# Two decoder layers on one core: finer signals at stage hand-overs, and merged rows turned in two steps

## The reference

```python
for l in range(DEPTH):
    h = rms_norm(x, norm_mix[l])
    # projections of h; y_a: block attention, y_b: state space layer + GLU
    o_g = gated_delta_rule(q_g, k_g, v_g, log_decay, beta)
    o_g = rms_norm(o_g, gdn_norm[l]) * silu(z_g)
    y_c = o_g @ w_up_gdn[l]
    merged = sigmoid(gate_a) * y_a + sigmoid(gate_b) * y_b + sigmoid(gate_c) * y_c
    x = x + merged @ w_out[l]
    x = x + cross_attention(rms_norm(x, norm_xa[l]), rms_norm(mem, norm_mem[l]), ...)
    h = rms_norm(x, norm_ffn[l])
    x = x + (swiglu(h, ...) if l % 2 == 0 else moe_swiglu(h, router, ...))
return rms_norm(x, norm_final)
```

## Time and profile before

| what | value |
|---|---|
| runs, median (lowest to highest) | 1812.19 us (1810.71 to 1813.0), 3 runs |
| the profiled execution | 1812.14 us |
| its span, first to last instruction | 1810.4 us |
| TensorE busy | 1739.8 us, 96% |
| VectorE busy | 1404.4 us, 78% |
| ScalarE busy | 1053.2 us, 58% |
| HBM moved | 239 GB/s over the span |

### The profile page before, as it was taken

The page is one execution under the profiler, slowest core; times in us unless marked ns, Lnnn a source line. Parts: engine busy times, 40 slices in busy tenths (PEclk is TensorE's granted clock), DMA queues, the critical chain, the costliest instruction groups (busy, mean ns, idle before and its releaser), DMA issues. The chain is left out here.

```text
span 1810.4 us, 23711 instructions
## 1 busy us (share of the span) xinstructions
PE 1739.8 (96%) x9509; PEld 1408.4 (78%) x9509; DVE 1404.4 (78%) x1765; ACT 1053.2 (58%) x1212; POOL 157.9 (9%) x211
## 2 busy tenths in 40 slices
PE   7999989999999999999899899999999999999997
PEld 5687767687888788776677788888888888888885
DVE  5678679665555467976877588989898989999996
ACT  4234555465443522454645667777777868777775
POOL 7330002000000215000010010000000000000020
PEclk9999999999999989999999999999999999999999
DMA  8334521357462544443214679999999999999993
GB/s 258 132 119 169 175 98 67 117 209 249 146 209 93 157 140 140 140 163 116 94 48 173 222 291 390 379 390 378 390 375 389 371 389 373 391 376 390 365 398 141
DMA packets 219155, 434.92 MB, mean 240 GB/s; under 512 B 19164, under 2 KB 61800, under 8 KB 219048
## 3 DMA queue, kind: packets, MB, share of 16 engines
q1 hardware_dynamic: 212664, 419.45, 64.2%
q0 software_dynamic: 3520, 11.76, 1.7%
q10 hardware_dynamic: 2864, 2.23, 0.4%
HBM read 422.93 MB, written 10.49 MB: 239 GB/s over the span
## 5 line engine op out<-in xcount | busy, mean ns | idle before, releaser
L1620 DVE TENSOR_TENSOR split_e<-ring,split_e 128x2048 fp32r<-128x2048 f32 x264 | 598.2, 2287 | 41.0 <-ACT split_e L1044 40.6
L1044 ACT ACTIVATE split_e<-ring 128x2048 fp32r<-128x2048 f32 x264 | 503.2, 1919 | 150.0 <-PE bank L3077 127.2
L3075 PE MATMUL bank<-split_e,fx_e 128*128 128x512 f32 x704 | 278.7, 396 | 2.0 <-DVE fx_e L2391 2.0
L3077 PE MATMUL bank<-split_e,fx_e 128*128 128x512 f32 x704 | 274.8, 390 | 0.0
L3076 PE MATMUL bank<-split_e,fx_e 128*128 128x512 f32 x704 | 274.4, 390 | 0.0
L3075 PEld LDWEIGHTS bank<-split_e,fx_e 128*128 128x128 f32 x704 | 132.3, 188 | 28.2 <-DVE fx_e L2391 2.2
L3077 PEld LDWEIGHTS bank<-split_e,fx_e 128*128 128x128 f32 x704 | 132.2, 188 | 28.0
L3076 PEld LDWEIGHTS bank<-split_e,fx_e 128*128 128x128 f32 x704 | 132.4, 188 | 26.2
L3075 PE MATMUL bank<-split_e,f_actT_e 128*128 128x512 f32 x352 | 137.7, 391 | 1.8 <-DVE f_actT_e L2399 1.8
L3077 PE MATMUL bank<-split_e,f_actT_e 128*128 128x512 f32 x352 | 137.1, 389 | 0.0
L3076 PE MATMUL bank<-split_e,f_actT_e 128*128 128x512 f32 x352 | 137.0, 389 | 0.0
(11 more groups left out here) (633 smaller groups left out, 3381.6 us busy)
## 6 DMA issues: line engine op xcount, KB each, us to landing
ring<-in_moe_w_gate SPq DMA_DIRECT2D x40, 2048.0 KB, 13.4
ring<-in_moe_w_up SPq DMA_DIRECT2D x40, 2048.0 KB, 13.5
ring<-in_moe_w_down SPq DMA_DIRECT2D x40, 2048.0 KB, 13.4
ring<-in_w_in SPq DMA_DIRECT2D x28, 2048.0 KB, 7.9
ring<-in_ffn_w_gate SPq DMA_DIRECT2D x11, 1024.0 KB, 5.4
ring<-in_ffn_w_up SPq DMA_DIRECT2D x11, 1024.0 KB, 7.9
ring<-in_ffn_w_down SPq DMA_DIRECT2D x11, 1024.0 KB, 8.7
ring<-in_ssm_w_glu SPq DMA_DIRECT2D x8, 1024.0 KB, 6.2
```

The costliest lines, as they stand in the source:

```text
L1044: nc.scalar.activation(split_e[j % NBUF][:, HI, :], ring[:, s * PIECE + i * HGRP:s * PIECE + (i + 1) * HGRP], ACT.Copy).then_inc(split_hi, 1)
L1620: V.tensor_tensor(split_e[j % NBUF][:, LO, :], ring[:, s * PIECE + i * HGRP:s * PIECE + (i + 1) * HGRP], split_e[j % NBUF][:, HI, :].bitca ...
L3075: mm(bank, a[HI], w[HI], start=first, stop=False)
L3077: return mm(bank, a[LO], w[HI], start=False, stop=last_one)
```

## The change

At five hand-overs a wait for a whole set of results becomes waits for its parts, or a product gets banks of its own:

- The first chunk of the dense layer goes into banks 2 and 3 instead of 0 and 1, so that the second chunk needs no wait for a bank (`first_two`).
- The last down product waits for the first tile's activations alone before its first half, multiplies its last group bank by bank, and signals after each bank; the additions to x follow bank by bank.
- In layer 1 the fourth addition to x comes before both multiplications by the gain, and the two follow together.
- The first expert's gather signals after its first bank, and ScalarE copies that bank then.
- VectorE signals the remainders of each bank of gathered rows by itself, for every expert, and TensorE waits for the first before the first half of the gate product and for the second before its other half.

Behind the delta rule VectorE reads the first up product before the remainder of the second tile, the last memory product moves forward, and the merged rows are turned in two steps. The counter `xo_ps` gets three more steps a dense layer, so its later values come from `xo_before`.

```diff
-                            nc.scalar.activation(f_th[t], B[t][:, 0:FC], ACT.Tanh, scale=half_rstd[:, t:t + 1]).then_inc(gu_th, 1)
+                            nc.scalar.activation(f_th[t], B[2 + t if head else t][:, 0:FC], ACT.Tanh, scale=half_rstd[:, t:t + 1]).then_inc(gu_th, 1)
...
-                        act.wait_ge(he_ps, n + 1)
                         for b in range(2):
+                            if n == 0 and b == 0:
+                                act.wait_ge(rl_ps, l // 2 + 4)
+                            else:
+                                act.wait_ge(he_ps, n + 1)
...
                 turned_rest(0)
                 normed(1)
-                turned_rest(1)
-                unit_split_lo(l, U_OUT, range(2))
-
-                for i, turn in enumerate(UP_ORDER):
-                    n_, t = turn // 2, turn % 2
+
+                def up_turn(i):
+                    n_, t = UP_ORDER[i] // 2, UP_ORDER[i] % 2
                     dve.wait_ge(up_ps, 8 * l + 4 + i + 1)
                     tmp = up_tmp[i % 2]
                     V.scalar_tensor_tensor(tmp, gates[:, t, 2 * D + n_ * 512:2 * D + (n_ + 1) * 512], 1.0, B[i % 2][:, :],
                                            ALU.add, ALU.mult).then_inc(up_used, 1)
                     dve.wait_ge(up_used, 8 * l + 4 + i + 1)
                     m = merged[:, t, n_ * 512:(n_ + 1) * 512]
-                    last = V.tensor_tensor(m, m, tmp, ALU.add)
-                    if i < 2:
-                        unit_split_lo(l, U_OUT, [2 + i])
-                last.then_inc(mg_ready, 1)
-                for b in range(4):
+                    V.tensor_tensor(m, m, tmp, ALU.add).then_inc(mg_ready, 1)
+
+                def merged_rest(b):
                     dve.wait_ge(x_hi, xs_base(l) + X_MG + b + 1)
                     V.tensor_tensor(merged_r[LO][:, 2 * b:2 * b + 2, :], B[4 + b][:, :].rearrange("p (c n) -> p c n", n=SEQ),
                                     merged_r[HI][:, 2 * b:2 * b + 2, :].bitcast(F32), ALU.subtract).then_inc(x_lo, 1)
+
+                up_turn(0)
+                turned_rest(1)
+                for i in range(3):
+                    unit_split_lo(l, U_OUT, [i])
+                    up_turn(i + 1)
+                merged_rest(0)
+                merged_rest(1)
+                unit_split_lo(l, U_OUT, [3])
+                merged_rest(2)
+                merged_rest(3)
                 unit_split_lo(l, U_OUT + 1, range(2))
...
-                    if l % 2 == 1 and i >= 2:
-                        dve.wait_ge(gain_in, 32)
-                        dve.wait_ge(xo_used, 4 * l + i + 1)
-                        dve.wait_ge(xo_ps, 4 * (l + 1))
+
+                if l % 2 == 1:
+                    dve.wait_ge(gain_in, 32)
+                    for t in range(NT):
+                        dve.wait_ge(xo_used, 4 * l + 3 + t)
                         V.tensor_tensor(xg[:, t, :], x[:, t, :], gain_bc, ALU.mult).then_inc(h_gain, 1)
...
-                    dve.wait_ge(split_used, 6 * NCH * (experts_before(l) + 1) + UNIT_SPLITS * (l + 1))
                     for i in range(4):
                         n_, t = i // 2, i % 2
+                        dve.wait_ge(*((xo_ps, xo_before(l) + 5 + i) if i < 3 else
+                                      (split_used, 6 * NCH * (experts_before(l) + 1) + UNIT_SPLITS * (l + 1))))
                         xs = x[:, t, n_ * 512:(n_ + 1) * 512]
                         V.tensor_tensor(xs, xs, B[4 + i][:, :], ALU.add).then_inc(y_added, 1)
...
-                        last.then_inc(fx_ready, 1)
+                            last.then_inc(fx_ready, 1)
...
                     if t == 0:
-                        memory_values(1, [6])
+                        memory_values(1, [6, 7])
                     if t == 1:
                         up(U_UPG, g_r, 8 * l + 4, None, [1], UP_ORDER)
                     pe.wait_ge(x_lo, xs_base(l) + X_G + t + 1)
                     up(U_UPG, g_r, 8 * l + 4, None, [0] if t == 0 else [2, 3], UP_ORDER)
-                memory_values(1, [7])
-
+
+                def turn_merged(b, t):
+                    for i in range(2):
+                        k = 2 * b + i
+                        last = tr(B[4 + b][:, i * SEQ + t * P:i * SEQ + (t + 1) * P], merged[:, t, k * P:(k + 1) * P], ident[:, :])
+                    return last
+
+                pe.wait_ge(mg_ready, 4 * l + 3)
+                for b in range(2):
+                    turn_merged(b, 0)
+                    turn_merged(b, 1).then_inc(mg_ps, 1)
+                turn_merged(2, 0)
+                turn_merged(3, 0)
+                pe.wait_ge(mg_ready, 4 * (l + 1))
+                turn_merged(2, 1).then_inc(mg_ps, 1)
+                turn_merged(3, 1).then_inc(mg_ps, 1)
                 pe.wait_ge(up_used, 8 * (l + 1))
-                pe.wait_ge(mg_ready, l + 1)
-                for b in range(4):
-                    for i in range(2):
-                        for t in range(NT):
-                            k = 2 * b + i
-                            last = tr(B[4 + b][:, i * SEQ + t * P:i * SEQ + (t + 1) * P], merged[:, t, k * P:(k + 1) * P], ident[:, :])
-                    last.then_inc(mg_ps, 1)
                 for n_ in range(2):
...
-                    for t, (t0, t1) in enumerate(tiles):
-                        for n_ in range(2):
-                            last = split_product(banks[n_][t][:, :], [src[:, a, i, t0:t1] for a in (HI, LO)],
-                                                 [w[:, a, n_ * 512:(n_ + 1) * 512] for a in (HI, LO)],
-                                                 first and i == 0, last_one and i == 1)
+                    for j in range(4):
+                        n_, t = (j // 2, j % 2) if last_one and i == 1 else (j % 2, j // 2)
+                        if last_one and i == 0 and j == 2:
+                            pe.wait_ge(actT_ready, last_one)
+                        t0, t1 = tiles[t]
+                        last = split_product(banks[n_][t][:, :], [src[:, a, i, t0:t1] for a in (HI, LO)],
+                                             [w[:, a, n_ * 512:(n_ + 1) * 512] for a in (HI, LO)],
+                                             first and i == 0, bool(last_one) and i == 1)
+                        if last_one and i == 1 and j < 3:
+                            last.then_inc(xo_ps, 1)
                     last.then_inc(split_used, 1)
...
-                        pe.wait_ge(actT_ready, at(c, NT - 1))
+                        pe.wait_ge(actT_ready, at(c, 0 if last_one else NT - 1))
                         for i in range(2):
                             down_group(g0 + down_at(c, i), NCH - 1 if last_one else 0, i, f_actT, [[B[4], B[5]], [B[6], B[7]]],
-                                       tiles, first, last_one)
+                                       tiles, first, at(c, NT - 1) if last_one else 0)
...
-                            gate_up_group(g0 + gu_at(c, i), c, i, fx, B[0:2], tiles,
-                                          (lambda t: pe.wait_ge(act_ready, at(c, t) - NT)) if i == 0 and not first_of_all(c) else None)
+                            gate_up_group(g0 + gu_at(c, i), c, i, fx, B[2:4] if head else B[0:2], tiles,
+                                          (lambda t: pe.wait_ge(act_ready, at(c, t) - NT)) if i == 0 and not first_two(c) else None)
...
+                            if n == 0 and k == KD // 2 - 1:
+                                last.then_inc(rl_ps, 1)
...
-                                    pe.wait_ge(fx_ready, 4 * fx_before(l) + n + 1)
+                                    pe.wait_ge(fx_ready, 4 * fx_before(l) + 2 * n + 1)
                                 bank_free(bank_turn(n, c, 0))
                                 input_group("g", n, c, 0, gate_bank(n, c))
                                 if full and prev is not None:
                                     flip(*prev)
+                                if c == 0:
+                                    pe.wait_ge(fx_ready, 4 * fx_before(l) + 2 * n + 2)
```

More of the change, by code:

```diff
@@ L493, in hybrid_trunk, with xo_before @@
         UP_ORDER = (0, 2, 1, 3)
+        def xo_before(l):
+            return 4 * l + 3 * ((l + 1) // 2)
         def multiplied(l, j):
@@ L503, in multiplied @@
                     U_WK: (xk_ps, 8 * l + 2), U_WV: (xk_ps, 8 * l + 4), U_WQ: (xk_ps, 8 * l + 8),
-                    U_WO: (xo_ps, 4 * l + 4)}[j]
+                    U_WO: (xo_ps, xo_before(l) + 4)}[j]
         def slot(j):
@@ L2216, in _ @@
                     n_, t = i // 2, i % 2
-                    dve.wait_ge(xo_ps, 4 * l + i + 1)
+                    dve.wait_ge(xo_ps, xo_before(l) + i + 1)
                     xs = x[:, t, n_ * 512:(n_ + 1) * 512]
@@ L2225, in _ @@
                         ffn_rest(i - 2)
-                    if l % 2 == 1 and i >= 2:
-                        dve.wait_ge(gain_in, 32)
-                        dve.wait_ge(xo_used, 4 * l + i + 1)
-                        dve.wait_ge(xo_ps, 4 * (l + 1))
+                if l % 2 == 1:
```

(11 more changed lines are left out.)

## The result

| kernel | median (lowest to highest) | runs |
|---|---|---|
| before | 1811.61 us (1810.71 to 1813.0) | 4 |
| after | 1796.2 us (1793.88 to 1796.64) | 4 |

The ratio is 0.9912, 95% interval 0.9895 to 0.9929: faster by 15.4 us, where 13.3 were forecast. The profiled execution took 1795.93 us with a span of 1794.2, 16.2 shorter than the span before.

A forecast was written before the change was run, and what follows sets the result against it. TensorE was taken as the bound, busy 50.00 of 50 us in the expert stage, with its largest waits at hand-overs between stages. Gains 6.66 + 1.87 + 2.06 + 1.14 + 1.59 = 13.32 took 1812.14 to 1798.8 us, range 1795.0 to 1804.5.

The forecast's parts named there:

- Behind the delta rule: Up turn 1 to output projection, both layers: turn 2 starts 1.78 us earlier, output projection 3.33 us earlier per layer.
- Rival (a): Behind the delta rule VectorE becomes the bound and only the first wait goes: 1801.9 us; chance 0.10.
- Dense head: First chunk of the dense feed-forward: chunk 1 starts without waiting for its bank, 1.87 us gained.
- Dense tail: End of the dense layer to layer 1's first projection: 2.06 us gained, 0.34 of it at the first wait.
- Gains: End of layer 1's cross-attention: fourth addition ahead of both multiplications is seen 1.14 us earlier.
- Gather: Gather for expert 0: first expert product starts 1.59 us earlier, at 1045.04, where the gather ends at 1044.62.
- Low clock: After layer 1's start and around the router: stretches may shift 2.8 us either way each, no sign.
- Rival (c): Both low-clock stretches get longer by 2.8 us each: 1804.4 us; chance 0.06.
- Experts: Expert stage from about 1046 us: its length should stay and only its start can move.
- (b): Experts' weight loads set the stage's end; gain behind the cross-attention (1.14 + 1.59) given back: 1801.6 us; chance 0.06.
- (d): Expert loop settles into a worse rhythm, slower than before: up to 1839.8 us; chance 0.04.
- (e): Hand-overs do not open, as a counter lets waiters through only at its last step: 1812 us; chance 0.02.

The follow-up runs named there:

- splits_first: Changed kernel, but VectorE again reads the first up product after the second half's remainder and two weight splits; 1800.52 us.
- one_step: Changed kernel, but TensorE turns all 16 tiles of the merged rows in one go after the fourth sum; 1799.69 us.
- after_third: The changed kernel, unchanged, measured a third time; 1796.08 us.
- before_again: The kernel before, unchanged, run once more for a second trace; 1811.93 us (one run).
- joints_only: Changed kernel with the functions behind the delta rule (up_turn, merged_rest, turn_merged) put back as before; 1803.64 us.
- delta_only: Kernel before with only the functions behind the delta rule (up_turn, merged_rest, turn_merged) as changed; 1804.99 us.
- early_norms: Changed kernel with the four row-norm products ahead of the 32 small products at a layer's start; 1795.11 us.
- norms_rest: Changed kernel with row norms ahead of the small products and the first gathered bank's remainder ahead of the token weights; 1794.59 us.
- fill_router: Changed kernel with 13 more 128x512 products at the router, results unused; 1799.08 us.
- norms_rest_fill: norms_rest with 13 more 128x512 products at the router, results unused; 1797.53 us.

## Why the prediction was right

**Behind the delta rule**, 3.33 a layer: measured 3.38 and 3.43. Both halves of the working hold: 1.78 for the first wait (1.86 by splits_first), 1.55 for the rest (1.46 by one_step). The fourth split and the remainders came in time, and the moved memory product cost nothing: from one fixed product ahead of it to the first up product pass 5.02 us, before 5.01. The wait of 0.20 in the transposes stands in the working too, between 363.7 and 363.9. Rival (a), VectorE as the bound, would have lost the second half; it is out.

**Dense head**, 1.87: 2.09 - 0.23 = 1.86. Another 0.1 us is saved inside chunk 1 in every kernel with the banks, and in none without; I had no term for it.

**Dense tail**, 2.06 with 0.34 for the first wait: 10.91 - 8.81 = 2.10, of it 0.33 at the first wait. **Gains**, 1.14: 61.72 - 60.47 = 1.25; the remaining wait is 0.3.

**Gather**, 1.59, with the first product 0.42 behind the gather's end. after_third, whose gather took 5.43, nearly the 5.54 on which the working rested, shows 0.42, and 2.01 - 0.42 = 1.59. Where the gather took 6.2 us or more the wait vanishes and the first product starts 0.24 before the gather's modelled end, so there the joint gives 2.25. In the first pair of traces the first expert product came only 1.12 nearer to the gather's start, because the gather itself was 1.13 longer.

**Low clock.** I allowed 2.8 us either way for each of the two stretches, with no sign. The traces spread by 1.5 us at layer 1's start (19.69 to 21.21) and by 2.1 from the router to the first expert product (13.88 to 15.94 with the joint open), for like programs on either side of the change. The rule of the Trainium skill that I cited (TensorE: Matmul & The Clock Gate, Part 1: The HAM clock gate), that the chip judges TensorE's activity on a grid that does not start with the kernel, is borne out as far as it goes: one program met the fall of the clock at different points, with 0.61 and 0.87 in the same window. Rival (c) shows in no trace: the two stretches of the changed kernel were never longer than 21.14 and 15.94, where the kernel before took 21.21 and 16.57 in the trace of the prediction.

**Experts.** From the 13th expert product to the last one ahead of the wait at the end pass 740.43 us in the changed kernel and 740.43 before. Rivals (b) and (d) are out, and (e) by every joint.

**What was missed.** With the gather at 1.59 the joints measured here add up to 13.6; the three medians of the changed kernel lie 15.4, 13.8 and 16.6 below their own kernel before, 15.2 on average. The traces account for such a difference. Between the two traces of the kernel before and the three of the changed one the span differs by 14.9 on average: 6.8 behind the delta rule, 4.1 in the dense layer, 1.3 at the gains, 1.5 from the router to the first expert product, 0.8 in the first twelve expert products (all of it from the low clock in before_again), 0.7 at the end of the experts, and -0.3 in the stretches from the program's start and from layer 1's start to the first up product. So that the gain is 2 us above the forecast is in part chance, namely where the clock fell; the end of the experts is the largest part that has no term in the prediction.

Before, TensorE waited there 1.8 and 1.7 for the last remainder, in the two traces; in the changed kernel 1.0, 0.9 and 0.9; in joints_only and delta_only, each with half of the change, 0.9; in splits_first, with nearly all of it, 1.5. The length goes with ScalarE's copy of one of the last weights, as the kernel before and delta_only show (timeline):

```profile
1779.02 3.72 ACT L1044 ACTIVATE split_e<-ring 128x2048 fp32r<-128x2048 f32 x2 [1.36 <-DMA ring<-in_moe_w_down]
...
1791.97 0.50 PE L3075 MATMUL bank<-split_e,f_actT_e 128*128 128x512 f32 x1 [1.79 <-DVE f_actT_e L2399]
```

```profile
1770.45 1.92 ACT L1044 ACTIVATE split_e<-ring 128x2048 fp32r<-128x2048 f32 x1 [1.40 <-DMA ring<-in_moe_w_down]
...
1783.40 0.50 PE L3088 MATMUL bank<-split_e,f_actT_e 128*128 128x512 f32 x1 [0.95 <-DVE f_actT_e L2405]
```

The copy waits for a load to land, and the product that ends TensorE's wait follows 12.95 us later in both, as in before_again, splits_first and the first trace of the changed kernel. So where the wait was above 0.95 the landing came later against TensorE's products. Why it did is open, and whether the change moves it or something that differs from run to run; no run tested it. The step of the prediction that was too strong is that the stage's length "should stay": its loop did, its last 10 us did not.

## What to carry to other kernels

Read each hand-over from the wait list, and work it out from the two instructions on either side: each such term was right to about 0.1 us, the gather's where the gather was as quick as in the trace that it was worked out from, and they add up when each sits at its own place on the path. Judge such gains by the distance between fixed instructions in two traces rather than by the medians, and take a second trace of the unchanged kernel first, to learn which stretches move by themselves. A gain read from a stretch of low clock can come out otherwise: early_norms gave half of what such a stretch promised. And when an instruction moves forward, look at what waits behind it: in norms_rest the later token weights cost more than the earlier remainder gave.

## What the hardware did unexpectedly

The granted clock fell while TensorE was issuing without a gap: in the changed kernel's trace the 32 small products (128x8) at layer 1's start took 4.58 us instead of 3.64, and the mean granted clock over 626 to 639 was 0.61. Nor did 8 wide products between the router's small ones keep it up: it was 0.50 over 1023 to 1025 in fill_router and over 1019 to 1031 in norms_rest_fill (means 0.89 and 0.64). In every trace, beside the program's start and end, the clock fell at these two places, among small products and waits, but where in them and for how long differed between executions of one program. In before_again and delta_only it fell once more, among the first expert products, which are wide and came without a gap, but stand behind a wait of 2.01.
